# A mixture-of-experts step on one NeuronCore: rows stationary and weights moving in experts 1 to 14, three of eight chunks of gate and up in three f32r passes

## The reference, cut to what matters

```python
h2 = rmsnorm(x, g_ffn)
# combine: for each row two experts of its best group, with weights
for e in range(16):
    he = silu(h2 @ w_gate[e]) * (h2 @ w_up[e])        # 1024 -> 256, twice
    moe = moe + combine[..., e:e+1] * (he @ w_down[e])  # 256 -> 1024
y = rmsnorm(x + moe, g_final)
```

## Time and profile before

| | |
|---|---|
| median of 3 runs | 437.52 us (434.93, 437.52, 439.68) |
| the profiled execution | 435.72 us; its span from first to last instruction 433.6 us |
| TensorE busy, weight loads | 413.9 us (95%), 364.1 us (84%) |
| VectorE, ScalarE, GpSimd busy | 273.2 (63%), 197.8 (46%), 126.3 us (29%) |
| DMA | 91.36 MB, mean 211 GB/s |
| mean granted TensorE clock | 0.994 of full speed |

### The profile page before, as it was taken

One profiled execution on the slowest core, in us unless ns is written; L12 is line 12 of the kernel. 1 busy time (PEld: TensorE's weight loads), 2 busy tenths in 40 slices (PEclk: granted clock), 3 DMA queues, 4 the chain that ended last, 5 costly groups with the idle time before them and its releaser, 6 DMA issues.

```text
span 433.6 us, 7776 instructions
## 1 busy us (share of the span) xinstructions
PE 413.9 (95%) x2919; PEld 364.1 (84%) x2919; DVE 273.2 (63%) x655; ACT 197.8 (46%) x485; POOL 126.3 (29%) x209
## 2 busy tenths in 40 slices
PE   6899999999999999999999999999989999999991
PEld 3687999997876886788887799999989999999981
DVE  2756430805759898635346898755566777776974
ACT  5566230705565766332222734444544555555632
POOL 2012000200034325151000323333334555554443
PEclk9999999999999999999999999999999999999997
DMA  7951704406000049923223789899999989986121
GB/s 250 323 182 50 231 2 135 169 2 202 2 1 3 0 155 418 373 97 147 97 98 129 245 322 421 335 403 379 355 339 341 374 332 386 364 321 251 59 89 47
DMA packets 32073, 91.36 MB, mean 211 GB/s; under 512 B 11200, under 2 KB 11712, under 8 KB 27942
## 3 DMA queue, kind: packets, MB, share of 16 engines
q1 hardware_dynamic: 20790, 71.97, 44.4%
q0 software_dynamic: 11248, 18.93, 12.3%
HBM read 86.38 MB, written 26.01 MB: 259 GB/s over the span
## 4 chain that ended last, share of the span: by engine, by line
PE 78%; DMA 7%; DVE 6%; ACT 4%; issue 3%; POOL 0%; SPq 0%; DVEq 0%; ACTq 0%; POOLq 0%
PE ps L1201 23%; PE ps L829 10%; PE ps L831 9%; PE ps L830 9%; DMA region_w<-in_w_down 5%; PE ps L1218 3%; PE ps L1219 3%; PE ps L1223 3%; PE ps L1194 3%; PE ps L993 2%; PE ps L1135 2%; PE ps L958 2%; DMA region_x<-in_x_prompt 1%; PE ps L976 1%; PE ps L1122 1%
## 5 line engine op out<-in xcount | busy, mean ns | idle before, releaser
L1201 PEld LDWEIGHTS ps<-region_p,region_a 128*128 128x128 f32 x512 | 58.3, 192 | 1.0 <-DVE region_p L2042 0.4
L1201 PE MATMUL ps<-region_p,region_a 128*128 128x128 f32 x512 | 58.5, 275 | 0.0
L831 PE MATMUL ps<-region_a_r,region_w_r 128*128 128x288 f32 x192 | 56.5, 295 | 0.0
L829 PE MATMUL ps<-region_a_r,ring_r 128*128 128x288 f32 x128 | 40.6, 317 | 0.0
L830 PE MATMUL ps<-region_a_r,ring_r 128*128 128x288 f32 x128 | 37.7, 295 | 0.0
L831 PEld LDWEIGHTS ps<-region_a_r,region_w_r 128*128 128x128 f32 x192 | 36.0, 188 | 0.0
L1592 ACT ACTIVATE region_p<-ps,gffn_sb 128x128 f32<-128x128 f32 x116 | 31.6, 384 | 7.7 <-PE ps L1194 7.7
L1613 ACT ACTIVATE region_t<-ps 128x256 f32<-128x256 f32 x16 | 6.1, 384 | 57.8 <-PE ps L1201 57.8
L1201 PEld LDWEIGHTS ps<-region_p,region_w 128*128 128x128 f32 x256 | 29.1, 192 | 1.8 <-issue 1.6
L702 POOL DMA_INDIRECT region_x<-h_rows,lists x13 | 16.7, 1283 | 47.3 <-DVE slot_w L2145 47.3
L1201 PE MATMUL ps<-region_p,region_w 128*128 128x128 f32 x256 | 29.3, 275 | 1.2 <-DMA region_w<-in_w_down 1.2
(11 more groups left out here) (365 smaller groups left out, 1020.1 us busy)
## 6 DMA issues: line engine op xcount, KB each, us to landing
region_a<-in_w_gate SPq DMA_DIRECT2D x8, 1024.0 KB, 9.3
region_a<-in_w_up SPq DMA_DIRECT2D x8, 1024.0 KB, 17.5
region_a<-in_w_down SPq DMA_DIRECT2D x8, 1024.0 KB, 18.5
region_w<-in_w_in SPq DMA_DIRECT2D x2, 2048.0 KB, 10.1
region_w<-in_w_out SPq DMA_DIRECT2D x2, 2048.0 KB, 7.9
ring<-in_w_gate SPq DMA_DIRECT2D x4, 1024.0 KB, 8.6
ring<-in_w_up SPq DMA_DIRECT2D x4, 1024.0 KB, 17.2
ring<-in_w_down SPq DMA_DIRECT2D x4, 1024.0 KB, 13.2
```

What stands on the lines that cost most here:

```text
L829: pe.matmul(out, lhs_hi, rhs_hi, start=first, stop=False)
L831: return pe.matmul(out, lhs_lo, rhs_hi, start=False, stop=last)
L1201: ins = pe.matmul(ps[:, 2 + b, (first + c) * P:(first + c + 1) * P], w[:, k, c * P:(c + 1) * P], xT[:, b, k, :], start=(k == 0), stop=(k = ...
```

## The change

Expert 0 and expert 15 stay as they are. In experts 1 to 14 (`mixed`):

- Gate and up (`gate_up_mixed`): the rows are stationary, the weights move, 256 columns per call; chunks 3 to 7 in f32, chunks 0 to 2 (`NF` = 3) in three f32r passes. The result is then by rows, not by features, so TensorE transposes the gated rows (`transpose_he`) between the two halves of the down product of the expert before.
- The rows of chunks 0 to 2 get a high part from ScalarE (`rows_hi`) and a remainder from VectorE (`rows_lo`). The gate and up weights of these chunks get a high part from ScalarE (`gu_his(i+2)`, two copies of 768, behind `wd_his(i+1)` and waiting for `ring_loaded` of expert i+2) and a remainder from VectorE (`gu_los(i+2)`, in place). `POOL_FROM` is 768 = 3 x 256, so the part of `gu_lo_part` that GpSimd would take is empty.
- `he_out` becomes one product; the high part and the remainder are made from the transposed rows (`he_hi_out` on ScalarE, `he_lo_out` on VectorE). One of the two down remainders of experts 1 to 13 goes to GpSimd (`wd_lo_half`).
- `count_overflow` moves from iteration 0 to 2 and `place_overflow` from 1 to 3, both at the end of VectorE's iteration; `g_final` is loaded in iteration 4 instead of 2.
- In iteration 0 VectorE evicts chunks 4 to 7 of the next rows instead of 0 to 3. Several semaphores are merged, with the same events behind each wait (left out below, as are the overflow case's).

```diff
 RING = 4
+NF = 3
+POOL_FROM = 768
 NOWHERE = 1024
...
             return wd_hi_last if isinstance(i, int) and i == E - 1 else wd_hi_two[:, i % 2]
+        he_tok = region_t[:, 0:512].rearrange("p (b f) -> p b f", b=2)
+        ring_r = [ring0_r[:, :], region_a_r[:, 0:6144], region_a_r[:, 6144:12288], region_w_r[:, 0:6144]]
+        wgu_sb = [r[:, 0:2 * WB].rearrange("p (a k f) -> p a k f", a=2, k=KC) for r in ring]
+        wgu_part = [[r[:, a * WB:a * WB + NF * FE] for a in range(2)] for r in ring]
+        wgu_lo = [[r[:, a * WB:a * WB + NF * FE] for a in range(2)] for r in ring_r]
+        wgu_hi = [[region_v_r[:, 0:NF * FE], region_v_r[:, 2304:2304 + NF * FE]],
+                  [region_w_r[:, 6144:6144 + NF * FE], region_w_r[:, 7168:7168 + NF * FE]]]
+        xT_hi = region_p_r[:, :].rearrange("p (b k s) -> p b k s", b=2, k=KC)
         wd_lo = [r.rearrange("p (c n) -> p c n", c=FC) for r in
...
         hT_pair = w_hi_extra[:, :].rearrange("p (k b t) -> p k b t", k=KC, b=2)
+        xT_lo = w_hi_extra[:, :].rearrange("p (b k s) -> p b k s", b=2, k=4)
         w_out_hi = [region_p_r[:, 0:D], region_p_r[:, D:2 * D], region_x_r[:, 0:D], region_x_r[:, D:2 * D], ring0_r[:, 4096:5120], ring0_r[:, 5120:6144],
...
                     load_down((i - 1) % RING, expert_at(i - 1 + RING))
-                if i == 2:
+                if i == 4:
                     sp.wait_ge(routed, 1)
-                    sp.dma_start(gfin, g_final.rearrange("(a d) -> a d", a=1).to_broadcast([P, D])).then_inc(gfin_loaded, 16)
+                    sp.dma_start(gfin, g_final.rearrange("(a d) -> a d", a=1).to_broadcast([P, D])).then_inc(gains_loaded, 16)
             sp.wait_ge(down_done, 2 * (E - RING))
...
                 rows_to(ys_v, N_SAMPLE, lists[:, i % LISTS, 3:4], yf[:, i % 2, :], stored)
+            def wd_lo_half(i):
+                pool.wait_ge(wd_hi_ready, FC * i + 2)
+                pool.tensor_tensor(wd_lo[i % RING][:, 1, :], wd_sb[i % RING][:, 1, :], wd_hi(i)[:, 1, :].bitcast(F32),
+                                   ALU.subtract).then_inc(lo_by_pool, 1)
+            def gu_lo_part(i):
+                r = slice(POOL_FROM, NF * FE)
+                pool.wait_ge(gu_hi_ready, 2 * i)
+                pool.tensor_tensor(wgu_lo[i % RING][1][:, r], wgu_part[i % RING][1][:, r], wgu_hi[i % 2][1][:, r].bitcast(F32),
+                                   ALU.subtract).then_inc(lo_by_pool, 1)
             gather_first()
...
                     gather_acc(i + 1)
+                if 1 <= i + 1 <= E - 3:
+                    wd_lo_half(i + 1)
+                if POOL_FROM < NF * FE and 3 <= i + 2 < E - 1:
+                    gu_lo_part(i + 2)
             pool.wait_ge(routed, 1)
...
                 ins.then_inc(signal, 1)
-            def down_split(u, i, bank):
+            def gate_up_mixed(slot, b, i, signal):
+                hi, lo = wgu_hi[slot % 2], wgu_lo[slot]
+                for a in range(2):
+                    out = ps[:, 2 + b, a * FE:(a + 1) * FE]
+                    for k in range(NF, KC):
+                        pe.matmul(out, xT[:, b, k, :], wgu_sb[slot][:, a, k], start=(k == NF), stop=False)
+                    if a == 0:
+                        pe.wait_ge(xlo_ready, i)
+                        pe.wait_ge(gu_lo_ready, i)
+                    elif POOL_FROM < NF * FE and not (isinstance(i, int) and i < 3):
+                        pe.wait_ge(lo_by_pool, 2 * i - 3)
+                    for k in range(NF):
+                        f = slice(k * FE, (k + 1) * FE)
+                        ins = three_passes(out, xT_hi[:, b, k, :], xT_lo[:, b, k, :], hi[a][:, f], lo[a][:, f], False, k == NF - 1)
+                ins.then_inc(signal, 1)
+            def transpose_he(u, i):
+                pe.wait_ge(he_ready, i + 1)
+                for c in range(FC):
+                    ins = pe.transpose(ps[:, 6 + u % 2, FE + c * P:FE + (c + 1) * P], he_tok[:, u % 2, c * P:(c + 1) * P], ident[:, :])
+                ins.then_inc(heT_full, 1)
+            def down_split(u, i, bank, between=None):
                 b, w_hi = u % 2, wd_hi(i if isinstance(i, int) else u)
...
                     ins.then_inc(down_done, 1)
+                    if half == 0 and between is not None:
+                        between()
             def first_rows():
...
                     pe.wait_ge(idx_ready, i + n + EARLY + (1 if first and n == 0 else 0))
+                    if n == EARLY and not (isinstance(it, int) and i <= 1):
+                        pe.wait_ge(he_lo_ready, i)
                     slot_lists((u + n) % RING * EPG + it + (u + n) // RING, (u + n) % RING)
                     pe.wait_ge(xT_dve, i + 1)
-                pe.wait_ge(xT_act, i + 1)
+                pe.wait_ge(xT_act, i + 1 if first else i)
                 pe.wait_ge(ring_loaded[u], it * 48 + 48)
-                gate_up(u, b, up_full)
+                if isinstance(it, int) and i == 1:
+                    pe.wait_ge(xhi_ready, 1)
+                if first or left == 0:
+                    gate_up(u, b, up_full)
+                else:
+                    gate_up_mixed(u, b, i, up_full)
                 if isinstance(it, int) and i == 1:
...
                         pe.wait_ge(state_evac, 1)
-                    pe.wait_ge(he_ready, i)
-                    if not (isinstance(it, int) and i == 1):
+                    if isinstance(it, int) and i == 1:
+                        pe.wait_ge(he_ready, 1)
+                    else:
+                        pe.wait_ge(heT_hi, i - 1)
                         pe.wait_ge(added, i - 1)
                     pe.wait_ge(wd_lo_ready, i)
-                    down_split((u - 1) % RING, i - 1, 4)
+                    if not isinstance(it, int) or 2 <= i <= E - 2:
+                        if POOL_FROM == NF * FE or (isinstance(it, int) and i == 2):
+                            pe.wait_ge(lo_by_pool, i - 1)
+                        else:
+                            pe.wait_ge(lo_by_pool, 2 * i - 4)
+                    down_split((u - 1) % RING, i - 1, 4, lambda: transpose_he(u, i))
                 if left == 1:
                     pe.wait_ge(idx_ready, E + EARLY + 1)
-                    pe.wait_ge(he_ready, i + 1)
+                    pe.wait_ge(heT_hi, i)
+                    pe.wait_ge(he_lo_ready, i + 1)
                     pe.wait_ge(wd_lo_ready, i + 1)
...
                     act.copy(wd_hi(i)[:, c, :], wd_sb[i % RING][:, c, :]).then_inc(wd_hi_ready, 1)
+            def gu_his(i):
+                act.wait_ge(ring_loaded[i % RING], 48 * (i // RING + 1))
+                if i >= 2:
+                    act.wait_ge(up_full, i - 1)
+                for a in range(2):
+                    act.copy(wgu_hi[i % 2][a], wgu_part[i % RING][a]).then_inc(gu_hi_ready, 1)
+            def mixed(i):
+                return 1 <= i < E - 1
+            def rows_hi(i):
+                b = i % 2
+                for k in range(NF, 4):
+                    rows_out(b, k)
+                for k in range(NF):
+                    ins = act.activation(xT_hi[:, b, k, :], ps[:, 0, k * P:(k + 1) * P], ACT.Copy, scale=gffn_sb[:, k:k + 1])
+                ins.then_inc(xhi_ready, 1)
+            def he_hi_out(i):
+                act.wait_ge(heT_full, i)
+                act.copy(he_hi[:, i % 2], ps[:, 6 + i % 2, FE:2 * FE].rearrange("p (c s) -> p c s", c=FC)).then_inc(heT_hi, 1)
             act.wait_ge(h2T_dve, NT)
             wd_his(0)
+            gu_his(1)
             def silu(i):
...
                     act.wait_ge(xg_transposed, i + 2)
-                    for k in range(4 if i == 0 else 0, KC):
-                        ins = rows_out((i + 1) % 2, k)
-                    ins.then_inc(xT_act, 1)
+                    if mixed(i + 1):
+                        rows_hi(i + 1)
+                    if i >= 1:
+                        for k in range(4 if mixed(i + 1) else 0, KC):
+                            ins = rows_out((i + 1) % 2, k)
+                        ins.then_inc(xT_act, 1)
+                    if mixed(i):
+                        he_hi_out(i)
                     if i < E - 2:
                         wd_his(E - 1)
+                    if mixed(i + 2):
+                        gu_his(i + 2)
             act.activation(warm[:, 0:1], ones[:, 0:1], ACT.Sqrt)
...
             def rows_out(b):
-                return dve.tensor_tensor(xT[:, b, 0:4, :], ps[:, 0, :].rearrange("p (k s) -> p k s", k=4),
-                                         wide(gffn_sb[:, 0:4], [P, 4, P]), ALU.mult)
+                return dve.tensor_tensor(xT[:, b, 4:8, :], ps[:, 1, :].rearrange("p (k s) -> p k s", k=4),
+                                         wide(gffn_sb[:, 4:8], [P, 4, P]), ALU.mult)
             dve.tensor_scalar(oh_last[0:N_SAMPLE, :], iota_one[0:N_SAMPLE, :], rm[0:N_SAMPLE, PT, e0:e0 + 1], None,
-                              ALU.is_equal).then_inc(oh_last_ready, 1)
+                              ALU.is_equal).then_inc(onehot_late, 1)
```

(40 more changed lines are left out.)

70 lines of the change are left out of this document (35 added, 35 removed).

## The result

448.79 us (median of four runs, 446.95 to 450.01) against 437.14: the ratio is 1.0281, with a 95% interval of 1.0241 to 1.0321. The change makes the kernel slower by 2.4 to 3.2%. The forecast was 439.0, in a range of 430 to 448; the time lies just above that range. The profiled execution took 450.01 us.

What follows compares the result with a forecast made beforehand. TensorE was taken to set the pace, with the DMA engines nearly full and hidden. Terms +2.6 - 0.9 + 1.7 - 2.0 + 0.3 = +1.7 us gave 437.4 profiled, 439.2 on the runs' scale; time 439, range 430 to 448.

Steps and rivals of the forecast that it cites:

- TensorE's prices: Gate and up per expert: f32 0.214 us apart, f32r 0.12; net -0.48 us per expert, period 10.50.
- U(3): End of gate and up of expert 3 (U(i): of expert i), forecast at 285.1, within 0.1 us of before.
- 1 us lands on VectorE: Experts 8 to 14: GpSimd's subtraction blocks VectorE for 1 us per period, half its turn beside PSUM reads and waits.
- the period of 10.7 in experts 8 to 14: Between 10.50 (nothing blocked) and 11.6 (all blocked), 10.7 us per expert: -2.0 us over seven experts.
- VectorE's own sum: Experts 8 to 14: VectorE's instructions add up to 9.5 us per expert, against 8.3 before.
- rival B: VectorE becomes the bound, GpSimd's remainder against one-hot and two-input subtractions: period 11.6, 446 us; chance 0.17.
- the wait at expert 3: TensorE waits 3.1 us for he_out(3), behind gu_los(4) and count_overflow on VectorE; U(4) +2.6.
- rival C: Weights pace every expert, 10.8 us or more, 441.2; TensorE's clock may halve after waits, up to 445; chance 0.17.
- the wait of 3.6 at expert 6: TensorE waits 3.6 us for he(6), behind ScalarE's copies held for expert 7's down weights; U(7) +3.4.
- L(7): Landing of expert 7's down weights, forecast 322, between 318 (no wait) and 326; before 323.06.
- the end: Last expert keeps its 64 instructions, TensorE runs the last two transposes ahead of it: +0.3 us.
- rival A: The gain is kept: weights land some 4 us earlier, waits at experts 3 and 7 go; 431.3 us, chance 0.23.

Runs made afterwards that it cites:

- Run two: Changed kernel with count_overflow and place_overflow ahead of the gate/up remainders in VectorE's order: 446.90 us, ratio 1.0238 to the kernel before.
- run one: Changed kernel with GpSimd's subtraction back on VectorE, which makes both down remainders: 439.77 us, ratio 1.0076 to the kernel before.
- run four: Changed kernel with overflow steps moved ahead and GpSimd's subtraction put where VectorE waits and reads PSUM: 440.87 us, ratio 1.0118 to the kernel before.
- run five: run four plus down loads counted on a semaphore of their own: 441.98 us, ratio 1.0125 to the kernel before.
- ten: run five with experts 4 to 15 loading only chunks 0 to 4 of gate and up: 432.06 us, ratio 0.9888 to the kernel before.

## Why the prediction was wrong

**Right: TensorE's prices.** f32 0.216 apart (forecast 0.214), f32r 0.118 (0.12), period 10.53 (10.50), the wait of expert 1 1.36 (1.55), U(3) counted from U(0) within 0.2 of the forecast, experts 5 and 6 -0.90 (-0.9). From the rounded steps in the earlier trace rows the line for f32r gives 0.116 and not 0.119; the term of 0.12 does not hang on it.

**Failed: "1 us lands on VectorE", the period of 10.7 in experts 8 to 14.** This was the mis-sized term: 2.86 us landed, and the period was 12.33 in experts 10 to 13. VectorE's own sum was right (9.5 forecast, 12.33 - 2.86 = 9.47 measured). What failed is the schedule: I put GpSimd's turn 2 to 4 us after U, half of it where VectorE waits or reads PSUM. Two turns of after, ahead of U(6) = 325.74 and behind U(7) = 336.27:

```profile
324.91 2.39 POOL L762 TENSOR_TENSOR region_a_r<-region_a,region_q_r 128x1024 fp32r<-128x1024 f32 x1
...
326.19 0.42 DVE L2253 TENSOR_TENSOR region_t<-region_t,ps 128x256 f32<-128x256 f32 x1 [2.22 <-ACT region_t L1707]
...
333.53 1.02 POOL L718 DMA_INDIRECT out_y_prompt<-region_x,lists  x1 [5.08 <-DVE region_x L2317]
...
339.53 2.40 POOL L762 TENSOR_TENSOR region_w_r<-region_w,region_q_r 128x1024 fp32r<-128x1024 f32 x1
...
339.99 2.63 DVE L2136 TENSOR_TENSOR region_v<-iota_one,rm 128x640 bf16<-128x640 f32 x1
```

In experts 5 and 6 the turn came 0.8 us before U, fell into VectorE's wait and its PSUM reads, and cost nothing: the period was 10.53. From the next turn on GpSimd stores two outputs first. That turn begins 3.3 us after U(7), when the PSUM reads are all but over, and meets the one-hot. The delay repeats: the stores wait for VectorE's finished rows (L2317), so a late VectorE makes the next turn late too (5.1 us after U(8), 5.9 after U(9) and U(10)), and it meets the one-hot each time until the last one-hot is made, and then a step of the root (2.58 and 2.57 us instead of 0.22). GpSimd's subtraction took 2.37 where I took 2.1. That is rival B, with a dearer price than its 11.6: 0.27 are GpSimd's longer turn, and 0.5 that the one-hot was held 0.6 us before GpSimd's recorded start. The Trainium skill ("SBUF — State Buffer", "SBUF: two separate sides") makes the pair of ports an exclusive lock for a VectorE instruction with two SBUF inputs against a GpSimd instruction that reads SBUF; the runs agree in 3.67, 1.74 and 0.81 us for the one-hot beside GpSimd's whole subtraction, its half and none. I had the rule and the rows for it, and then halved its price by a schedule that no row showed.

**Failed in size: the wait at expert 3.** 4.43 us against 3.1: the same lock held gu_los(4) for 1.8 us. Run two shows count_overflow's place in it (2.74 with the steps moved), run one the lock's (2.96 without GpSimd). I had the half clock only in rival C; it cost 3.1 us here.

**Did not come: the wait of 3.6 at expert 6.** Its mechanism is real (run four: 6.90 us of ScalarE held for down weights, TensorE 3.46). The term that failed is L(7): I took 322 and said that 318.4 or less would leave no wait. The down weights of expert 7, issued at 308.79, 8.7 us later than in before, took 8.9 us instead of 23.0 and landed at 317.74; TensorE asked for the product of expert 6 at about 328. The delay at expert 3 is time that the loads had and TensorE had not (the DMA share was down to 0.73 and 0.68 from 294 to 298 us). I added two delays of which the first covers the second.

**Missed: the end.** +2.75 for expert 15 against +0.3. 2.21 of it are a wait for the product of expert 14:

```profile
412.12 2.57 DVE L2311 SCALAR_TENSOR_TENSOR root<-root 128x1 f32<-128x1 f32 x1
...
418.22 2.35 DVE L2291 TENSOR_TENSOR region_a_r<-region_a,region_q_r 128x1024 fp32r<-128x1024 f32 x2
420.48 2.36 DVE L2291 TENSOR_TENSOR region_w_r<-region_w,ring_r 128x1024 fp32r<-128x1024 f32 x2
```

VectorE was held once more (the step of the root) and has the four down remainders of experts 14 and 15 ahead of that product, which begins at 422.75. In run one, where GpSimd has no turn, the wait is 0.77; in run two, where it has one, 2.21 again.

**Not weighed: the loads.** I wrote that two resources were nearly full, and then gave rival A 0.23 for keeping the gain. Runs five and ten show what that left out: run five has TensorE at 10.53 us an expert up to U(10), loses the lead to late rows, and does not lose it with 9 MB fewer. An estimate from the rows of four and five: at the 377 to 385 GB/s of their fullest experts (share 0.99 and 1.00) 51.5 MB take 134 to 137 us, and thirteen experts at 10.53 take 136.9, so next to nothing is left to make up a stall. From U(0) to U(13) before has 143.0 us, and no version with all bytes has less. That no order of the loads and gathers could keep the pace is not shown.

## What to carry to other kernels

Before work is moved to GpSimd, look at what VectorE runs at that hour: two SBUF inputs there mean that one engine stands still until the other's instruction is over, and a period that it lengthens can lock the two together. Where a hidden resource is nearly full (a share of 0.93 and 0.94 here), price the gain by that resource first: the bytes over the best rate that a stage shows, against the stretch as it is to be, and what is left to make up a stall. And when several delays are added up along one chain, ask which of them the earlier ones cover.
